# Two of three down parts of each FFN as seven products of half blocks

## The reference

```
def swiglu_ffn(x, norm, w_gate, w_up, w_down):
    h = rms_norm(x, norm)
    return (jax.nn.silu(h @ w_gate) * (h @ w_up)) @ w_down
...
x = x + 0.5 * swiglu_ffn(x, ffn1_norm[l], ffn1_w_gate[l], ffn1_w_up[l], ffn1_w_down[l])
```

## Time and profile before

| | |
|---|---|
| median of 3 runs | 3165.3 us (3165.1 to 3166.48) |
| the profiled execution | 3162.72 us |
| its span in the profile | 3160.9 us |
| TensorE busy | 3110.3 us |
| VectorE busy | 2060.4 us |
| ScalarE busy | 1617.1 us |
| DMA, mean over the span | 132 GB/s |

### The profile page before, as it was taken

The page is one execution under the profiler, slowest core; times in us unless marked ns, Lnnn a source line. Parts: engine busy times, 40 slices in busy tenths (PEclk is TensorE's granted clock), DMA queues, the critical chain, the costliest instruction groups (busy, mean ns, idle before and its releaser), DMA issues.

```text
span 3160.9 us, 37974 instructions
## 1 busy us (share of the span) xinstructions
PE 3110.3 (98%) x15130; PEld 2571.4 (81%) x15130; DVE 2060.4 (65%) x3190; ACT 1617.1 (51%) x2515; POOL 320.2 (10%) x358
## 2 busy tenths in 40 slices
PE   9999999999999999999999999999999999999998
PEld 7789877778887888788987777887889877787887
DVE  7665778745476657756578855457575666785656
ACT  6443568644354436534467754345353556564434
POOL 2110020100021001201001100002010100021100
PEclk9999999999999999999999999999999999999999
DMA  9844341322399456957233322369572554289552
GB/s 262 206 111 110 100 117 61 107 80 87 100 240 221 118 127 180 232 134 174 67 108 93 90 87 80 94 186 233 135 171 71 109 89 68 67 237 220 118 130 69
DMA packets 297586, 417.95 MB, mean 132 GB/s; under 512 B 15424, under 2 KB 199232, under 8 KB 297408
## 3 DMA queue, kind: packets, MB, share of 16 engines
q1 hardware_dynamic: 234592, 298.62, 31.6%
q0 software_dynamic: 62240, 116.02, 20.1%
...
## 4 chain that ended last, share of the span: by engine, by line
PE 79%; DVE 9%; DMA 7%; ACT 4%; issue 1%; POOL 0%; DVEq 0%; SPq 0%; ACTq 0%; POOLq 0%
PE bank L656 24%; PE bank L668 14%; PE bank L661 14%; PE bank L670 10%; PE bank L663 10%; DMA k_xraw<-in_ffn_w_gate 4%; DVE k_wl L867 2%; PE bank L1489 1%; PE bank L1107 1%; DMA k_xraw<-in_ffn_w_up 1%; PE bank L1538 1%; PE bank L1522 1%; ACT k_wh L842 1%; DMA k_xraw<-in_w_gate 1%; PE bank L1791 1%
## 5 line engine op out<-in xcount | busy, mean ns | idle before, releaser
L867 DVE TENSOR_TENSOR k_wl<-k_raw,k_wh 128x1024 fp32r<-128x1024 f32 (+1 forms) x314 | 369.9, 1178 | 272.5 <-ACT k_wh L842 270.8
L842 ACT ACTIVATE k_wh<-k_xraw 128x1024 fp32r<-128x1024 f32 (+1 forms) x302 | 300.2, 995 | 446.4 <-PE bank L668 211.9
L842 ACT ACTIVATE k_wh<-k_raw 128x1024 fp32r<-128x1024 f32 (+1 forms) x314 | 320.9, 1022 | 399.8 <-PE bank L668 298.8
L867 DVE TENSOR_TENSOR k_wl<-k_xraw,k_wh 128x1024 fp32r<-128x1024 f32 (+1 forms) x302 | 343.0, 1143 | 176.0 <-ACT k_wh L842 175.4
L656 PE MATMUL bank<-k_xh,k_wh 128*128 128x512 f32 x968 | 395.8, 409 | 0.0
L668 PE MATMUL bank<-k_xh,k_wl 128*128 128x512 f32 x968 | 378.6, 391 | 0.1
L661 PE MATMUL bank<-k_xl,k_wh 128*128 128x512 f32 x968 | 377.7, 390 | 0.0
L670 PE MATMUL bank<-k_wl,k_S 128*128 128x512 f32 (+1 forms) x732 | 272.7, 373 | 15.4 <-ACT k_sc L1137 13.0
L656 PE MATMUL bank<-k_wh,k_S 128*128 128x512 f32 (+1 forms) x732 | 274.4, 375 | 0.0
L656 PE MATMUL bank<-k_h,k_wh 128*128 128x512 f32 x696 | 272.4, 391 | 0.0
L668 PE MATMUL bank<-k_h,k_wl 128*128 128x512 f32 x696 | 271.1, 390 | 0.0
...
## 6 DMA issues: line engine op xcount, KB each, us to landing
k_raw<-in_w_in SPq DMA_DIRECT2D x153, 512.0 KB, 3.7
k_xraw<-in_ffn_w_up SPq DMA_DIRECT2D x65, 512.0 KB, 8.6
k_xraw<-in_ffn_w_gate POOLq DMA_DIRECT2D x54, 512.0 KB, 9.7
k_xraw<-in_ffn_w_gate SPq DMA_DIRECT2D x51, 512.0 KB, 7.1
k_xraw<-in_ffn_w_down SPq DMA_DIRECT2D x49, 512.0 KB, 4.4
k_xraw<-in_ffn_w_up POOLq DMA_DIRECT2D x30, 512.0 KB, 10.6
k_raw<-in_w_out SPq DMA_DIRECT2D x28, 512.0 KB, 3.4
k_raw<-in_ffn_w_gate POOLq DMA_DIRECT2D x22, 512.0 KB, 12.6
```

Of the source, the lines that this page charges most:

```text
L842: e.activation(self.pair[c.pair][0][:, 0:n], self.unit[c.src][:, 0:n], ACT.Copy).then_inc(*self.act.up(("wh", c.i)))
L867: e.tensor_tensor(lo[:, 0:n], self.unit[c.src][:, 0:n], hi[:, 0:n].bitcast(F32), ALU.subtract).then_inc(*self.dve.up(("wl", c.i), ("split" ...
```

## The change

Parts 0 and 1 of the down product become 2 x 2 block products as well, with seven half products each. A weight quarter is 512 rows (one block of hidden features) by 512 columns, an activation quarter is one block's features by 256 tokens, so the moving operand has 256 columns. The operands of the seven products (`DOWN_ORDER`) are quarters of the activations, kept whole in float32 in `k_hf`, or sums of them that VectorE makes in free buffers of `k_sc` (`dve_operand_sums`, L1239); ScalarE and VectorE split each anew (`act_operands`, L1213; `dve_operands`, L1222 and L1225) into two alternating pairs. Each half of a product's result is added straight onto a quarter of x, with its sign (`dve_down_sums`, L1262). Two results belong to two quarters of the output each; the orders of `where`, `first` and `last` and the sums of activations make one addition per result enough. The weights of a part are seven pieces of two chunks: B11, B21, B22 loaded, T1 = B12 + B11 by one adding transfer, T2 = B12 + B11 + B22 by two, T2 + B21 by one more, T3 = T2 - B11 on VectorE. The parts move behind P3 of blocks 2 and 4.

In gate and up, block 1's T1 is now T2 - B22 on VectorE, like that of later blocks, and its load and adding transfer go away. The transposed pieces of blocks 0 to 3 are copied to `k_hf` by ScalarE alone (L1179). In some forty places the tick offsets of queued pieces are different, in the mixers too. The last part (2) is as before.

```diff
+HALF = 0.53
...
-        out += [(b, "P6"), (b, "P2"), (b, "P7")] + [(b // 2 - 1, "down")] * (b % 2 == 0) + [(b, "P5")]
-        out += [(b + 1, "P1")] * (b + 1 < NB) + [(b, "P4"), (b, "P3")]
+        out += [(b, "P6"), (b, "P2"), (b, "P7"), (b, "P5")] + [(b + 1, "P1")] * (b + 1 < NB) + [(b, "P4"), (b, "P3")]
+        out += [(b // 2 - 1, "down")] * (b % 2 == 0)
...
+DOWN_ORDER = ("P1", "P2", "P6", "P5", "P7", "P3", "P4")
...
+            3: (("D0", "P7"), ("D0", "P3"), None, ("D0", "P4")),
+            5: (("D1", "P7"), ("D1", "P3"), None, ("D1", "P4")),
...
-        if b > 1:
+        if b > 0:
             out[begin1]["loads"].append((b, "B22", "B22"))
             at("P6")["loads"].append((b, "T1", None))
             at("P6")["post"].append((b, "T1", "T2", "B22", ALU.subtract, None))
...
+    for b, before in (("D0", 2), ("D1", 4)):
+        at = lambda n: out[b, n]
+        for n, piece in (("P1", "B11"), ("P2", "B21"), ("P3", "B22")):
+            at(n)["loads"].insert(0, (b, piece, piece))
+        out[before, "P4"]["loads"].append((b, "T2", "B12"))
+        out[before, "P4"]["adds"].append((b, "T2", "B11"))
+        out[before, "P3"]["adds"].append((b, "T2", "B22"))
+        at("P1")["loads"].append((b, "T1", "B12"))
+        at("P1")["adds"].append((b, "T1", "B11"))
+        at("P6")["post"].append((b, "T3", "T2", "B11", ALU.subtract, "B11"))
+        at("P6")["more"].append((b, "T2", "B21"))
+        for n in ("P2", "P3", "P4", "P5", "P7"):
+            at(n)["gone"].append((b, SOURCE[n]))
...
+            if b in ("D0", "D1"):
+                r0, nf = BLOCKS[2 * int(b[1]) + int(n[1]) - 1]
+                return wd, l, r0, nf // P, 512 * (int(n[2]) - 1) + 256 * h, 256
...
     def down(g):
-        last = g == NB // 2 - 1
-        if last and not keep:
+
+        nf = BLOCKS[2 * g][1] // P
+        at["down", g] = p.now
+        for name in DOWN_ORDER:
+            at["down", g, name] = p.now
+            cs = []
+            for s in weight_pieces(st, f"D{g}", name, steps_of[f"D{g}", name]):
+                cs.append(p.chunk(p.now, 2 * nf * HALF, nf, 256, ext=True, **s))
+                p.now += 2 * nf * HALF
+            banks = swapped(st, (4, 5) if name in ("P1", "P6", "P7", "P4") else (0, 1))
+            p.fill((st, "down", g, name), at["down", g, name], banks, cs)
...
+    def pe_down(self, e, st, part):
+
         nf = BLOCKS[2 * part][1] // P
-        steps = [(kb, m) for kb in range(2) for m in (0, 2, 4)] + [(0, 6), (1, 6)]
-        if not last:
-            steps = [(kb, q + m) for q in (0, 4) for kb in range(2) for m in (0, 2)]
-        for kb, m0 in steps:
+        for n, name in enumerate(DOWN_ORDER):
+            g = self.p.group[st, "down", part, name]
+            t = g.at
+            hi, lo = self.OP[n % 2]
+            for h, c in enumerate(g.chunks):
+                wh, wl = self.parts(c)
+                for m in range(2):
+                    cols = slice(m * P, (m + 1) * P)
+                    for k in range(nf):
+                        yield t
+                        t += HALF
+                        s = slice(256 * k, 256 * k + 256)
+                        end, spent = k == nf - 1, m == 1 and k == nf - 1
+                        marks = [("done", st, "down", part, name, h)] * spent + [("spent", c.i)] * spent
+                        self.three(e, self.bank[g.banks[h]][:, 256 * m:256 * m + 256], (hi[:, s], lo[:, s], (st, "O", part, name)), c,
+                                   wh[:, k, cols], wl[:, k, cols], True, name in ("P1", "P2", "P5") and k == m == 0, end,
+                                   g.after.need if spent and h else (), marks)
...
-                yield c.split + 2.4
+                yield c.split + 8.4
...
+    def down_source(self, st, part, name):
+
+        b, d = 2 * part + 2, self.at[st]["down", part]
+        h = lambda k, t: self.HF4[:, k, :, 256 * t:256 * t + 256]
+        pairs = self.ffn_tiles(b)
+        s, q = (self.SCW[[self.SC.index(x[0]) // 2 for x in pairs][i]].rearrange("p (k n) -> p k n", k=4) for i in (0, 3))
+        return {"P1": (h(0, 0), []), "P2": (h(1, 0), []), "P4": (h(1, 1), []),
+                "P6": (s, [(-6.0, q, h(1, 1), h(0, 1), ALU.subtract), (4.5, s, q, h(0, 0), ALU.add)]), "P5": (q, []),
+                "P7": (q, [(21.0, q, h(0, 0), h(0, 1), ALU.subtract)]),
+                "P3": (s, [(14.0, s, s, h(1, 0), ALU.subtract)])}[name]
...
+    def down_tick(self, st, part, n):
+
+        return self.at[st]["down", part] + (8.5 * (n - 1) + 0.9 if n > 1 else -10.7 + 2.2 * n)
...
+    def act_operands(self, e, st, part):
+        for n, name in enumerate(DOWN_ORDER):
+            src, sums = self.down_source(st, part, name)
+            yield self.down_tick(st, part, n)
+            if sums:
+                e.wait_ge(*self.dve.sig(("os", st, part, name, len(sums) - 1)))
+            elif name == "P5":
+                e.wait_ge(*self.dve.sig(("os", st, part, "P6", 0)))
+            else:
+                e.wait_ge(*self.act.sig(("hf", st, part, 3 if name == "P1" else 7)))
+            if n > 1:
+                e.wait_ge(*self.pe.sig(("done", st, "down", part, DOWN_ORDER[n - 2], 1)))
+            elif part:
+                e.wait_ge(*self.pe.sig(("done", st, "down", part - 1, DOWN_ORDER[5 + n], 1)))
+            hi = self.OP[n % 2][0].rearrange("p (k n) -> p k n", k=4)
+            e.activation(hi, src, ACT.Copy, scale=-1.0 if name == "P6" else 1.0).then_inc(*self.act.up(("xh", st, "O", part, name)))
...
+    def dve_operands(self, e, st, part):
+        for n, name in enumerate(DOWN_ORDER):
+            src, sums = self.down_source(st, part, name)
+            yield self.down_tick(st, part, n) + 0.4
+            e.wait_ge(*self.act.sig(("xh", st, "O", part, name)))
+            hi, lo = (x.rearrange("p (k n) -> p k n", k=4) for x in self.OP[n % 2])
+            if name == "P6":
+                e.scalar_tensor_tensor(out=lo, in0=src, scalar=-1.0, in1=hi.bitcast(F32), op0=ALU.mult,
+                                       op1=ALU.subtract).then_inc(*self.dve.up(("xl", st, "O", part, name)))
+            else:
+                e.tensor_tensor(lo, src, hi.bitcast(F32), ALU.subtract).then_inc(*self.dve.up(("xl", st, "O", part, name)))
+
+    def dve_operand_sums(self, e, st, part, name):
+
+        before = {"P7": "P5", "P3": "P6"}.get(name)
+        for i, (t, out, x, y, op) in enumerate(self.down_source(st, part, name)[1]):
+            yield self.at[st]["down", part] + t
+            if name == "P6":
+                e.wait_ge(*self.dve.sig(("h", st, 2 * part + 2, 3 - 2 * i)))
+                e.wait_ge(*self.act.sig(("hf", st, part, 7)))
+            else:
+                e.wait_ge(*self.dve.sig(("xl", st, "O", part, before)))
+            if i:
+                e.wait_ge(*self.dve.here())
+            e.tensor_tensor(out, x, y, op).then_inc(*self.dve.up(("os", st, part, name, i)))
...
+    def dve_down_sums(self, e, st, part):
+
+        scale = FFN[st][4]
+        X3 = self.X_.rearrange("p (k n) -> p k n", k=KD)
+        where = {"P1": (0, 0, 1), "P2": (0, 0, 1), "P6": (1, 0, -1), "P3": (1, 0, -1), "P5": (1, 1, -1), "P7": (1, 1, -1), "P4": (0, 1, 1)}
+        first, last = {"P1": "P2", "P6": "P3", "P5": "P7", "P4": "P4"}, {"P2": "P1", "P3": "P6", "P7": "P5"}
...
+        for name in DOWN_ORDER:
+            half_, tok, sign = where[name]
+            for t in range(2):
+                yield self.at[st]["down", part, name] + 4.24 * (t + 1) + 0.3
+                bank = self.bank[self.p.group[st, "down", part, name].banks[t]].rearrange("p (k n) -> p k n", k=2)
+                m = 4 * half_ + 2 * t
+                dst = X3[:, m:m + 2, 256 * tok:256 * tok + 256]
+                e.wait_ge(*self.pe.sig(("done", st, "down", part, name, t)))
+                if name in last:
+                    e.wait_ge(*self.dve.sig(("dn", st, part, last[name], t)))
+                elif part:
+                    e.wait_ge(*self.dve.sig(("dn", st, part - 1, first[name], t)))
+                else:
+                    for k in (m, m + 1):
+                        e.wait_ge(*self.sig(self.x_ready(st, k)))
+                e.scalar_tensor_tensor(out=dst, in0=bank, scalar=sign * scale, in1=dst, op0=ALU.mult,
+                                       op1=ALU.add).then_inc(*self.dve.up(("dn", st, part, name, t)))
...
```

152 lines of the change are left out of this document (84 added, 68 removed).

## The result

| | before | after |
|---|---|---|
| median | 3165.9 us (3165.1 to 3166.6, 4 runs) | 3128.1 us (3126.2 to 3130.9, 4 runs) |
| the profiled execution | 3162.72 us | 3130.85 us |

The ratio is 0.9881 (95% interval 0.9864 to 0.9898): 37.8 us less. Forecast were 27 us less, 3138 us, with a range of 3108 to 3176. The time lies in the range, but half of it came from a place that the prediction had put at nothing, and the down parts gave less than half of what it had expected of them.

What follows compares the result with a forecast made beforehand. The prediction took the number of matmuls times their spacing on TensorE as the bound. Matmuls -37 and waits +10 gave -27 us on 3162.7, 3136; the runs' median lies 2.6 us higher, so 3138 us, range 3108 to 3176.

Steps and rivals of the forecast that it cites:

- I take 0: FFN starts: two adding transfers fewer for block 1 gain nothing; some 20 us could be gained or lost.
- the late addition: First blocks of FFN 2: adding transfer issued at 955.11, landing at 977; forecast issue about 963 to 967, landing 971 to 978.
- The cheap case: Rival: 256-column matmuls run at 0.11 us, or the late add at FFN starts goes away; 3108 us or so, chance 0.12.
- The matmul term: Down parts: 336 matmuls of 256 columns at 0.119 us, 40.0 us against 43.7; 37 us less in ten parts.
- The rule of the Trainium skill: Weight loads overlap matmuls only across row groups: about 107 + 107 ns per 256-column matmul, some 280 us slower; rejected.
- The wait term: Down parts: TensorE waits 0 to 2 us a part for VectorE's remainders, taken as 1.0, 10 us in all.
- a part of 40 to 42 us: Sign that would show the forecast: P1 of the down product to its P4 takes 40 to 42 us.
- The count of 39 to 41 us: Down parts: VectorE's queue between first and last residual, 39.3 to 41.4 us of work against TensorE's 37.1 us.
- VectorE paces the parts: Rival: all 4.3 us of VectorE's surplus on the path, 44.3 us a part, 3165 to 3171 us; chance 0.12.
- The cost of nothing: DMA queues: 14 adds and 2 loads more per FFN, 44 us of transfers, share about 0.83, hidden by early requests.
- The rival's mechanism: Down parts: adds for T2 land late, one 4.8 us stall a part, 3186 us; chance 0.19.
- The bound of 9.1 us for attention: Attention: shifted offsets can gain at most TensorE's present waits there, 9.1 us; taken as 0.

## Why the prediction was right, and where it was wrong

**Right in number, by two errors.** Forecast -27, measured -37.8. The direction is the mechanism's doing; that the number is as near as it is, is luck, since the two errors have opposite signs. The sum was down parts -27, starts 0, offsets 0. It came out as starts -19 and all the rest -18, of which the down matmuls are -12. The first step that failed is "I take 0" at the FFN starts. The prediction held that the landing which releases GpSimd's queue would come near 962, that the late addition would be issued at 963 to 967 and that it would land as late as before; the landing came at 953, the late addition was issued at 956.52 and landed at 970.3. It had shortened the queue by the two adding transfers' own time, 5.8 us, and the queue was 11.3 us shorter. The cheap case had these 20 us in it, at a chance of 0.12 that it shared with another cause.

**The matmul term.** 40.0 us forecast, 336 x 0.120 = 40.3 measured, and 43.5 for the part before, not 43.7. That makes -32 instead of -37 us in ten parts. The rule of the Trainium skill that spoke against the change (TensorE: Matmul & The Clock Gate, Part 3) is not borne out at 256 columns: 3360 matmuls with a load each start 0.120 us apart, and by the rule it would be 0.214 us, an estimate. Its figure for a load of 128 columns (LDWEIGHTS), 107 ns, agrees with the one place where a load is exposed: beside a wait, where an interval is 0.22 us and not 0.12.

**The wait term.** 10 us forecast, and the profile shows 10.1 us, 6.3 of them at P5 on L1225, the line that the prediction named. The other 3.8 are at P6 on L1222, which it had not named, and at P7, which it had, there is none. But each shown 0.6 us costs 1.0 to 1.25 us, one of them 1.4. In FFN 2 a part is 41.6 us without a wait, 42.7 with one and 43.8 with two, each with 1.1 us of transposes, so the sign "a part of 40 to 42 us" did not hold either. The sixteen cost 18.5 us, not 10. This is the second step that failed: a term mis-sized by the price of a wait, not by its length. With both, -32 + 18.5 makes -14 us, near the -12 that the intervals in the trace give.

**VectorE.** The count of 39 to 41 us against 37 us of matmuls held: it is busy 98 to 99% of a part, and six remainders more a part put 78% of their time on the path, the slow stretches included. "VectorE paces the parts" was given 0.12 and is not what happened, but it is one instruction away, and the six waits that no reordering removed are its beginning.

**The transfers.** The cost of nothing held in the changed kernel, but thinly: ScalarE waits 4.4 us for a landing in the first part of FFN 2, and when the part became 1 to 2 us shorter this wait reached TensorE. The rival's mechanism was real; its place was not the T2 of a down part but the weights of the next block, held up on GpSimd's queue behind an addition that waits for VectorE.

**The offsets.** The bound of 9.1 us for attention held (2.7 and 2.4 us gained), and the last mixer's loss of 5.6 us was not foreseen, since the prediction looked only for what offsets could gain.
